# Spreading a bisection's sign passes over more steps of an attention mixer on one Trainium2 core

## Chip, cores and metric

One core of one Trainium2 chip runs the whole program. The metric is the time of one execution in device microseconds (us), median of several runs; lower is better.

## What is computed

The reference is two transformer blocks in sequence, in fp32, on 1024 tokens of width 1024 with a context of 256 tokens. The first block has two layers (latent attention, a depthwise convolution, a Fourier branch and a spatial gate). The second has a hybrid mixer with three kinds of attention, a memory attention and a convolutional feed-forward. The change lies in the third kind of attention of the mixer: for each query an index score is computed against every earlier key, and only the 256 best keys are attended to.

```python
score = jnp.einsum('bqhk,bqh->bqk', jax.nn.relu(logits), iwb)
score = jnp.where(kpos[None, None, :] <= qpos[None, :, None], score, NEG)
_, idx = lax.top_k(score, topk)            # topk = 256
...
s = jnp.where(valid[:, None], s + bias, NEG)
p = jax.nn.softmax(s, axis=-1)
```

## The kernel before

The queries of the mixer are eight tiles of 128 (t = 0 to 7); tile t sees (t+1)*128 keys. The mixer runs as 64 steps. Step n belongs to branch n // 16 and, in it, to query tile (n % 16) // 2 and to one of two head pairs. Branches 0 and 1 (steps 0 to 31) are the difference attention, branch 2 (steps 32 to 47) is the dilated one, and branch 3 (steps 48 to 63) is the one with the selected keys. So steps 0, 1, 16, 17, 32, 33, 48 and 49 are the narrowest and 14, 15, 30, 31, 46, 47, 62 and 63 the widest.

Each engine has its own program, written out by hand, in which the steps follow one another; engines meet at semaphores. In one step n:

- TensorE (PE) multiplies the scores of step n (`scores2`, L934), transposes the probabilities of step n-1 (`turn2`, L945), runs **fillers** (projections for the next branch, L856 and L867, half of the output projection, L879), transposes the output of an earlier step back (`back2`, L972), and multiplies with the values of step n-1 (`values2`, L957 or L962).
- VectorE (DVE) adds the bias and takes the row maximum (`scored`, L2172), narrows the search (`narrow`, L2056 to L2071), adds the two maps of a head pair (`combine`, up to step 31) or scales them (`normalise`, L2195 and L2197, from step 32), and, up to step 32, divides the output of the step before (`divide`, L2210).
- ScalarE (ACT) copies transposes out of PSUM (`turned2`, L1145), takes the exponentials (`weigh`, L1560, two a step), copies fillers out, copies the output of the step before (with a root of its mean square up to step 32, `head_root`, L1568 to L1573), and counts signs (`count_signs`, L1604 and L1607). It also issues the DMAs of the bias strips, behind steps 16, 31, 46 and 47.

PE may issue the scores of a step before the softmax of the step before is done, since there are four PSUM banks for scores; fillers share two banks and transposes two more.

**The search.** The 256th largest score of every row is found by bisection on the bits of the number, in 33 passes. A pass of a tile is one ACTIVATE with the function Sign over the whole tile and its sum (L1607; pass 0 is L1604), and then four or so tiny VectorE instructions for all tiles of the group at once (`narrow`). The next pass needs the bound that the last one gave. Tiles 2 to 5 are the group "low" (widths 384, 512, 640 and 768), tiles 6 and 7 the group "high" (896 and 1024). In ACT's program tiles 2 and 3 are counted behind the first exponential of the step, and tiles 4 to 7 behind the second. VectorE narrows for pass n-1 in step n.

A pass used to come in every step: low in steps 0 to 32, high in steps 23 to 55. When a group is done, `keep_ranked` (L2108 to L2133) makes the mask of one tile out of the bound, one tile at a time, on VectorE alone and at the end of a step: it counts the scores above the bound, finds which of several equal scores are kept, by a running sum over parts of 256, and writes the mask over the scores. The table `RANKED_AT` says behind which step each tile is ranked: tiles 2, 3, 4 and 5 behind 34, 36, 38 and 40, tiles 6 and 7 behind 57 and 59. The masks are first read by `scored` of step 52 (tile 2), 54 (tile 3), 56, 58, 60 and 62.

Fillers stand in steps 0 to 47, in step 52 (the mean square of the memory tokens, L886) and from step 54 on. Steps 48 to 51 and 53 have none.

```python
for piece in FILLERS.get((n, 1), ()):
    filled(*piece)
...
keep_ranked(n)
if 1 <= n <= 32:
    divide(n - 1)
```

Of the kernel before, what the change touches and what calls it, by code (L numbers as in the profile page):

```python
# [205 lines left out]


SEARCHED = {"low": (2, 3, 4, 5), "high": (6, 7)}
SEARCH_AT = {"low": 0, "high": 23}
PASSES = 33  # L210
RANKED_AT = {34: 2, 36: 3, 38: 4, 40: 5, 57: 6, 59: 7}
MEM_STEP = 52
FILLERS = fillers()
INDEX_FILLERS = projections(0, ("k0", "q0", "k1", "q1", "v"))
# [51 lines left out]
class Psum:  # L266
# [20 lines left out]
    def at(self, key):  # L287
        return self.tensor[:, self.bank[key] * 512:8 * 512]
# [48 lines left out]
def program(nc, A, known):  # L337
# [94 lines left out]
    def sel(t):  # L432
        return view(SEL_AT[t], (t + 1) * P)
# [704 lines left out]
    def scalar_program(raw):  # L1138
# [452 lines left out]

        def count_signs(group, n, tiles):

            i = n - SEARCH_AT[group]
            if not 0 <= i < PASSES:
                return
            for t in tiles:
                j, x = t - 2, sel(t)
                out = signs_out[t % 2][:, 0:(t + 1) * P]
                e.wait_ge(*at(unread_signs.get(t % 2)))  # L1600
                unread_signs[t % 2] = ("counted", group, i, t)
                if i == 0:
                    e.wait_ge(*at(("causal", t)))
                    ins = act(out, x, ACT.Sign, accum_out=tally[:, j:j + 1])  # L1604
                else:
                    e.wait_ge(*at(("bound", group, i)))
                    ins = act(out, x, ACT.Sign, bias=bound[:, j:j + 1], scale=sense[:, j:j + 1],  # L1607
                              accum_out=tally[:, j:j + 1])
                ins.then_inc(*e.step(("counted", group, i, t)))
# [4 lines left out]
        for n in range(STEPS2 + 1):  # L1614
            if n >= 1:
                turned2(n - 1, 0)
            if n < STEPS2:
                weigh(n, 0)
            count_signs("low", n, (2, 3))
            for piece in FILLERS.get((n, 0), ()):  # L1620
                filled(*piece)
            if n >= 33:
                turned2(n - 1, 1)
            if n < STEPS2:
                weigh(n, 1)
            count_signs("low", n, (4, 5))
            count_signs("high", n, (6, 7))
            for piece in FILLERS.get((n, 1), ()):
                filled(*piece)
# [78 lines left out]
    def vector_program(raw):  # L1708
# [321 lines left out]
        v.tensor_scalar(subln8, vec("subln"), 1.0 - LAM_INIT, None, ALU.mult).then_inc(*e.step("subln8"))  # L2030
        def narrow(group, n):

            i = n - SEARCH_AT[group]
            if not 0 <= i < PASSES:
                return
            tiles = SEARCHED[group]
            g = slice(tiles[0] - 2, tiles[-1] - 1)
# [52 lines left out]
        def parts_of(t):  # L2090
            return [(a, min(256, (t + 1) * P - a)) for a in range(0, (t + 1) * P, 256)]

        def keep_ranked(n):

            if n not in RANKED_AT:
                return
            t = RANKED_AT[n]
            j, x, parts = t - 2, sel(t), parts_of(t)
# [37 lines left out]
        for t, i in INDEX_STEPS:  # L2136
            for m in range(2):
                h = 2 * i + m
                n = 8 * (t - 2) + h
# [81 lines left out]
        for n in range(STEPS2 + 1):  # L2221
            if n < STEPS2:
                scored(n, 0)
            narrow("low", n - 1)
            if n < STEPS2:
                scored(n, 1)
            narrow("high", n - 1)
            for piece in FILLERS.get((n, 0), ()):
                filled(*piece)
            if n < 32:  # L2230
                combine(n)
            elif n < STEPS2:
                normalise(n, 0)
                normalise(n, 1)
            for piece in FILLERS.get((n, 1), ()):
                filled(*piece)
            if n == MEM_STEP:
                e.wait_ge(*at("mem rr"))
                for k in range(KD):
                    stt(out=mem[:, k, :], in0=mem[:, k, :], scalar=vec("norm_memkv", k), in1=mem_rr, op0=ALU.mult,  # L2240
                        op1=ALU.mult).then_inc(*e.step(("mem h", k)))
# [3 lines that stand above are left out]
# [416 lines left out]
```

## Time and profile before

| what | value |
|---|---|
| median of 3 runs | 3642.03 us (3641.57 to 3643.51) |
| profiled execution, its own time | 3638.48 us |
| its span, first to last instruction | 3636.3 us |
| PE busy | 3475.0 us (96%) |
| PE weight loads | 1830.7 us (50%) |
| DVE busy | 1456.9 us (40%) |
| ACT busy | 1008.1 us (28%) |
| mean granted TensorE clock | 0.983 of full |

The profiled execution is 3.55 us below the median of the runs, and its time is 2.2 us above its span. The mixer's 64 steps lie between 1774.6 and about 2426.8 us from the span's start. Step starts used below are those of the first scores matmul of a step on PE.

### The profile page before, as it was taken

How to read it: one execution, taken by the hardware profiler on the slowest of the kernel's cores; microseconds unless marked ns; L12 is line 12 of the kernel's file. 1: busy time of each engine (PE TensorE's matmuls, PEld its weight loads, DVE VectorE, ACT ScalarE, POOL GpSimd, SP SyncE). 2: the span in 40 equal slices, each digit the busy share in tenths (PEclk: the TensorE clock that was granted, in tenths of full speed). 3: DMA queues.
4: the chain of work that ended last, by engine and by line, in shares of the span. 5: the costliest groups of instructions: out<-in, count | busy, mean ns of one | idle time of the engine just before them, and what ended most of it. 6: DMA issues, size and time to landing. Idle time of an engine off the chain costs nothing.

```text
span 3636.3 us, 31117 instructions
## 1 busy us (share of the span) xinstructions
PE 3475.0 (96%) x12466; PEld 1830.7 (50%) x12466; DVE 1456.9 (40%) x2652; ACT 1008.1 (28%) x2122; POOL 70.4 (2%) x91
## 2 busy tenths in 40 slices
PE   7999999999999999999999899899999999999998
PEld 3556555655456445444566455564544444444443
DVE  2056191123056351232443363652224555153433
ACT  4244112002244111112688745531211000000001
POOL 0000000010000000100000000000000000000000
PEclk9999999999999999999999999899999999999999
DMA  5100121130000101111100101111001111111111
GB/s 212 50 5 12 58 86 61 52 113 32 26 6 13 39 26 47 47 38 41 41 24 24 38 21 61 56 44 49 24 18 40 41 41 45 36 46 41 41 41 64
DMA packets 49901, 163.70 MB, mean 45 GB/s; under 512 B 5296, under 2 KB 8624, under 8 KB 49085
## 3 DMA queue, kind: packets, MB, share of 16 engines
q1 hardware_dynamic: 44890, 145.82, 11.5%
q10 hardware_dynamic: 4868, 15.91, 1.3%
q8 instruction: 98, 1.61, 0.2%
q14 instruction: 45, 0.37, 0.0%
HBM read 157.46 MB, written 11.32 MB: 46 GB/s over the span
## 4 chain that ended last, share of the span: by engine, by line
PE 86%; DVE 6%; ACT 6%; issue 1%; SPq 1%; DMA 0%; POOL 0%; DVEq 0%; ACTq 0%; POOLq 0%
PE ps L485 43%; PE ps L1086 14%; PE ps L856 5%; PE ps L576 4%; PE ps L867 2%; ACT sb L1607 2%; PE ps L599 2%; PE ps L755 2%; PE ps L588 2%; PE ps L879 1%; PE ps L934 1%; PE ps L945 1%; DVE sb L1795 1%; PE ps L841 1%; ACT sb L1560 1%; PE ps L962 1%
## 5 line engine op out<-in xcount | busy, mean ns | idle before, releaser
L485 PE MATMUL ps<-sb 128*128 128x512 f32 (+1 forms) x3856 | 1568.6, 568 | 13.6 <-ACT sb L1410 6.7
L485 PEld LDWEIGHTS ps<-sb 128*128 128x128 f32 x3856 | 733.7, 191 | 840.3 <-issue 820.9
L1145 ACT ACTIVATE sb<-ps 128x512 f32<-128x512 f32 (+11 forms) x706 | 349.2, 511 | 1434.0 <-PE ps L485 542.3
L1086 PE MATMUL ps<-sb 128*128 128x512 f32 x1232 | 529.9, 592 | 2.9 <-DVE sb L2353 2.9
L1086 PEld LDWEIGHTS ps<-sb 128*128 128x128 f32 x1232 | 233.9, 190 | 298.2 <-issue 292.7
L856 PE MATMUL ps<-sb 128*128 128x512 f32 x512 | 232.9, 603 | 0.0
L1187 ACT ACTIVATE sb<-sb 128x512 f32<-128x512 f32 x128 | 76.0, 613 | 479.7 <-DVE sb L1997 157.6
L1607 ACT ACTIVATE sb<-sb 128x384 int8<-128x384 f32 (+2 forms) x192 | 184.4, 963 | 1.0 <-DVE sb L2052 0.5
L1931 DVE SCALAR_TENSOR_TENSOR sb<-sb 128x1310 f32<-128x1310 f32 (+1 forms) x120 | 161.7, 1432 | 0.0
L576 PE MATMUL ps<-sb 96*128 96x512 f32 (+1 forms) x400 | 155.3, 523 | 5.2 <-ACT sb L1319 4.5
L856 PEld LDWEIGHTS ps<-sb 128*128 128x128 f32 x512 | 94.9, 193 | 108.3 <-issue 107.5
L1795 DVE TENSOR_REDUCE sb<-ps 128x1 f32<-128x1280 f32 (+1 forms) x72 | 98.9, 1373 | 97.4 <-PE ps L576 97.1
L1720 DVE SCALAR_TENSOR_TENSOR sb<-sb 128x512 f32<-128x512 f32 (+1 forms) x138 | 88.0, 706 | 110.8 <-ACT sb L1168 86.0
L2300 DVE TENSOR_TENSOR sb<-ps,sb 128x512 f32<-128x512 f32 x64 | 44.3, 691 | 216.6 <-PE ps L485 216.6
L867 PE MATMUL ps<-sb 128*128 128x256 f32 x512 | 118.5, 387 | 0.0
L1560 ACT ACTIVATE sb<-sb 128x128 f32<-128x128 f32 (+7 forms) x128 | 98.7, 771 | 62.2 <-DVE sb L2172 33.1
L576 PEld LDWEIGHTS ps<-sb 96*128 96x128 f32 x400 | 71.9, 192 | 78.8 <-issue 73.2
L867 PEld LDWEIGHTS ps<-sb 128*128 128x128 f32 x512 | 97.7, 195 | 18.9 <-issue 6.2
L588 PE MATMUL ps<-sb 128*128 128x128 f32 x656 | 99.5, 281 | 5.1 <-DVE sb L1812 2.1
L1319 ACT ACTIVATE sb<-ps,sb 128x1280 f32<-128x1280 f32 (+1 forms) x72 | 88.7, 1232 | 48.9 <-DVE sb L1795 48.7
L1997 DVE SCALAR_TENSOR_TENSOR sb<-ps,sb 128x512 f32<-128x512 f32 (+1 forms) x40 | 27.9, 697 | 176.2 <-PE ps L485 176.2
L945 PE MATMUL ps<-sb 128*128 128x128 f32 x432 | 70.9, 288 | 28.8 <-DVE sb L2210 18.7
(225 smaller groups left out, 2872.9 us busy)
## 6 DMA issues: line engine op xcount, KB each, us to landing
sb<-in_w_in SPq DMA_DIRECT2D x73, 512.0 KB, 3.3
sb<-in_w_ada SPq DMA_DIRECT2D x48, 512.0 KB, 4.6
sb<-in_w_up SPq DMA_DIRECT2D x44, 512.0 KB, 3.3
sb<-in_w_down SPq DMA_DIRECT2D x24, 384.0 KB, 3.0
sb<-in_w_out SPq DMA_DIRECT2D x16, 512.0 KB, 3.3
sb<-in_w_mkv SPq DMA_DIRECT2D x16, 512.0 KB, 3.3
rows_dram<-vec_dram ACTq DMA_DIRECT2D x1, 6906.0 KB
sb<-rows_dram ACTq DMA_DIRECT2D x6, 1024.0 KB, 5.3
```

Source lines behind the costliest of these rows:

```text
L485: ins = mm(ps[:, 0:tn], w[:, k, :], src(k, t0, tn), start=(k == 0), stop=(k == nk - 1))
L576: ins = mm(ps[:, b:b + w], qh[0:96, h % 2, t * P:(t + 1) * P], kh[0:96, h, keys0 + b:keys0 + b + w], start=True, stop=True)
L588: ins = transpose(ps[:, (j - g) * P:(j - g + 1) * P], prob[u % 3][:, j * P:(j + 1) * P], ident)
L856: ins = mm(ps[:, 0:512], weights[name][:, k, :], H2[:, k, 512 * c:512 * c + 512], start=(k == 0), stop=(k == KD - 1))
L867: ins = mm(ps[:, 0:256], H2[:, k, t * P:(t + 1) * P], w[k // 4][:, k % 4, :], start=(k == 0), stop=(k == KD - 1))
L945: ins = transpose(ps[:, (j - g) * P:(j - g + 1) * P], score_tile(n, m)[:, j * P:(j + 1) * P], ident)
L1086: ins = mm(ps[:, 0:512], stationary(k), moving(k), start=(first and k == 0), stop=(k == 3), skip_group_check=not first)
L1145: return act(out, in_, func, scale=scale)
L1560: act(tile, tile, ACT.Exp, bias=small[:, s:s + 1], scale=-1.0, accum_out=small[:, s + 1:s + 2]).then_inc(*e.step(("exp2", n, m)))
L1607: ins = act(out, x, ACT.Sign, bias=bound[:, j:j + 1], scale=sense[:, j:j + 1], accum_out=tally[:, j:j + 1])
L1795: v.tensor_reduce(small[:, s:s + 1], psum.at((l, "s", u))[:, 0:nk], AX.X, ALU.max, negate=True).then_inc(*e.step((l, "max", u)))
L1931: ins = stt(out=out, in0=src, scalar=w, in1=out, op0=ALU.mult, op1=ALU.add)
```

## The change

Two tables of step numbers replace the two first steps. Pass i of the low group now stands in step 4*i // 3 and pass i of the high group in step 12 + 4*i // 3, so a group has passes in three steps of four and none in the steps with n % 4 == 3. Low: steps 0, 1, 2, 4, 5, 6, ... 42. High: 12, 13, 14, 16, ... 54. The two groups leave out the same steps. The rankings of tiles 2 to 5 move to the ends of steps 45, 46, 48 and 50; those of tiles 6 and 7 stay. Nothing is added or taken away; the number of passes is 33 for both groups as before.

```diff
 SEARCHED = {"low": (2, 3, 4, 5), "high": (6, 7)}
-SEARCH_AT = {"low": 0, "high": 23}
 PASSES = 33
-RANKED_AT = {34: 2, 36: 3, 38: 4, 40: 5, 57: 6, 59: 7}
+SEARCH_AT = {group: {first + 4 * i // 3: i for i in range(PASSES)} for group, first in (("low", 0), ("high", 12))}
+RANKED_AT = {45: 2, 46: 3, 48: 4, 50: 5, 57: 6, 59: 7}
```

In `count_signs` and in `narrow` alike:

```diff
-            i = n - SEARCH_AT[group]
-            if not 0 <= i < PASSES:
+            i = SEARCH_AT[group].get(n)
+            if i is None:
                 return
```

The first place is ACT's program in step 20 (branch 1, tile 2), from its first exponential to the root of the output of step 19. Before:

```order
L1560 ACTIVATE sb<-sb 128x384
L1607 ACTIVATE sb<-sb 128x384
L1607 ACTIVATE sb<-sb 128x512
L1560 ACTIVATE sb<-sb 128x384
L1607 ACTIVATE sb<-sb 128x640
L1607 ACTIVATE sb<-sb 128x768
L1568 ACTIVATE sb<-ps,sb 128x128
L1571 ACTIVATE sb<-sb 128x1
L1573 ACTIVATE sb<-sb 128x1
```

The same place in the changed kernel:

```order
L1560 ACTIVATE sb<-sb 128x384
L1607 ACTIVATE sb<-sb 128x384
L1607 ACTIVATE sb<-sb 128x512
L1560 ACTIVATE sb<-sb 128x384
L1607 ACTIVATE sb<-sb 128x640
L1607 ACTIVATE sb<-sb 128x768
L1607 ACTIVATE sb<-sb 128x896
L1607 ACTIVATE sb<-sb 128x1024
L1568 ACTIVATE sb<-ps,sb 128x128
L1571 ACTIVATE sb<-sb 128x1
L1573 ACTIVATE sb<-sb 128x1
```

Two wide signs have come in front of the root; in step 19, just before, all four signs are gone.

The second place is VectorE's program between step 48 and step 49 (branch 3, tile 0; ISA is `scored`). Before, from the last scaling of step 48:

```order
L2195 RECIPROCAL sb<-sb 128x1
L2197 TENSOR_SCALAR sb<-sb 128x128
L2172 ISA sb<-ps,sb 128x128
L2172 ISA sb 128x1
L2172 ISA sb<-ps,sb 128x128
L2172 ISA sb 128x1
```

In the changed kernel, from the same scaling:

```order
L2195 RECIPROCAL sb<-sb 128x1
L2197 TENSOR_SCALAR sb<-sb 128x128
L2108 TENSOR_SCALAR sb<-sb 128x256 x2
L2108 TENSOR_SCALAR sb<-sb 128x128
L2108 TENSOR_SCALAR sb<-sb 128x256 x2
L2108 TENSOR_SCALAR sb<-sb 128x128
L2110 TENSOR_SCALAR sb<-sb 128x1
L2112 TENSOR_TENSOR sb<-sb 128x1
L2113 TENSOR_SCALAR sb<-sb 128x1
L2115 SCALAR_TENSOR_TENSOR sb<-sb 128x1
L2118 SCALAR_TENSOR_TENSOR sb<-sb 128x1
```

Thirteen rows more of the same ranking (tile 4) follow, up to L2133, before `scored` of step 49. The ranking of tile 5 stands in the same way between steps 50 and 51.

## Rows read from the trace of the kernel before

**Rows 1.** The page, part 1: busy time of each engine over the whole span
```profile
PE 3475.0 (96%) x12466; PEld 1830.7 (50%) x12466; DVE 1456.9 (40%) x2652; ACT 1008.1 (28%) x2122; POOL 70.4 (2%) x91
```
**Rows 2.** Busy time by stretch: steps 0-11, 12-15, 16-19, 20-23, 24-27, 28-31, 32-38
```profile
core 0: us, PE busy (x) PEld busy (x) DVE busy (x) ACT busy (x) POOL busy (x), PEclk, DMA share, GB/s
1774.60:1867.60 93.00, 88.96 (x391) 57.72 (x390) 38.40 (x162) 79.69 (x218) 0.29 (x1) 1.00 0.13 46
1867.60:1907.60 40.00, 38.65 (x169) 21.61 (x168) 19.66 (x52) 32.37 (x77) 0.00 (x0) 1.00 0.06 20
1907.60:1937.10 29.50, 28.06 (x107) 14.77 (x106) 9.90 (x52) 25.01 (x73) 0.00 (x0) 1.00 0.18 64
1937.10:1967.40 30.30, 29.56 (x137) 20.85 (x136) 13.08 (x52) 27.31 (x76) 0.00 (x0) 1.00 0.06 18
1967.40:2014.30 46.90, 37.71 (x178) 27.18 (x178) 18.43 (x72) 40.38 (x99) 0.00 (x0) 0.93 0.06 23
2014.30:2062.60 48.30, 42.23 (x169) 22.91 (x168) 21.73 (x68) 41.96 (x95) 0.00 (x0) 0.93 0.06 16
2062.60:2137.00 74.40, 73.78 (x329) 47.20 (x328) 33.30 (x149) 41.16 (x104) 0.00 (x0) 1.00 0.10 33
```
**Rows 3.** Busy time of the sign passes alone (L1607): steps 0-11, steps 44-47
```profile
1774.60:1867.60 93.00, 39.64 (x88) 1.00 0.13 46
2212.70:2267.80 55.10, 9.78 (x16) 1.00 0.15 51
```
**Rows 4.** Busy time by stretch: steps 25, 27, 29, 31, and the sum over 24-31
```profile
1974.50:1992.30 17.80, 13.43 (x58) 10.74 (x57) 5.79 (x21) 13.46 (x33) 0.00 (x0) 0.81 0.00 0
...
2000.00:2014.30 14.30, 10.98 (x46) 5.92 (x46) 5.93 (x19) 13.68 (x32) 0.00 (x0) 1.00 0.19 74
...
2021.60:2037.60 16.00, 13.11 (x48) 6.81 (x47) 6.44 (x19) 13.16 (x30) 0.00 (x0) 0.89 0.11 33
...
2045.70:2062.60 16.90, 13.75 (x51) 7.30 (x50) 7.03 (x19) 15.05 (x33) 0.00 (x0) 0.90 0.06 14
sum 95.20, PE 79.93 PEld 50.09 DVE 40.16 ACT 82.34 POOL 0.00; mean PE 9.99 PEld 6.26 DVE 5.02 ACT 10.29 POOL 0.00
```
**Rows 5.** Timeline, step 24 into 25: start, us, engine, line [idle <-releaser]
```profile
1977.79 1.23 ACT L1607 ACTIVATE sb<-sb 128x1024 int8<-128x1024 f32 x1
...
1980.08 0.20 ACT L1573 ACTIVATE sb<-sb 128x1 f32<-128x1 f32 x1
...
1980.39 0.41 DVE L2210 TENSOR_SCALAR sb<-ps,sb 128x128 f32<-128x128 f32 x1 [4.04 <-ACT sb L1573]
...
1980.85 0.47 PE L945 MATMUL ps<-sb 128*128 128x128 f32 x1 [3.80 <-DVE sb L2210]
```
**Rows 6.** Busy time by stretch: step 39 and step 41
```profile
2137.00:2155.90 18.90, 15.38 (x56) 6.92 (x54) 14.11 (x45) 5.22 (x11) 0.00 (x0) 0.91 0.05 15
...
2166.10:2187.10 21.00, 16.84 (x64) 8.07 (x62) 15.23 (x45) 5.76 (x13) 0.00 (x0) 0.84 0.10 26
```
**Rows 7.** Timeline of DVE: first and last row of the rankings of tiles 4, 5
```profile
2136.87 0.47 DVE L2108 TENSOR_SCALAR_CACHE_REDUCE sb<-sb 128x256 f32<-128x256 f32 x1
...
2146.47 0.49 DVE L2133 TENSOR_SCALAR sb<-sb 128x640 f32<-128x640 f32 x1
...
2165.75 0.47 DVE L2108 TENSOR_SCALAR_CACHE_REDUCE sb<-sb 128x256 f32<-128x256 f32 x1
...
2176.23 0.56 DVE L2133 TENSOR_SCALAR sb<-sb 128x768 f32<-128x768 f32 x1
```
**Rows 8.** Timeline of steps 48 to 52: ends of scalings, next `scored`, memory sum
```profile
2272.10 0.29 DVE L2197 TENSOR_SCALAR sb<-sb 128x128 f32<-128x128 f32 x1
...
2273.59 0.29 DVE L2172 CUSTOM_DVE_ANT_0 sb<-ps,sb 128x128 f32<-128x128 f32 x1 [1.21 <-PE ps L934]
...
2279.63 0.35 DVE L2197 TENSOR_SCALAR sb<-sb 128x256 f32<-128x256 f32 x1
...
2280.94 0.42 DVE L2172 CUSTOM_DVE_ANT_0 sb<-ps,sb 128x256 f32<-128x256 f32 x1 [0.95 <-PE ps L934]
...
2287.97 6.75 PE L886 MATMUL ps<-sb 128*128 128x256 f32 x16 [1.37 <-ACT sb L1647]
```

More of the change, by code:

```diff
@@ L2031, in narrow @@
         def narrow(group, n):
-            i = n - SEARCH_AT[group]
-            if not 0 <= i < PASSES:
+            i = SEARCH_AT[group].get(n)
+            if i is None:
                 return
```

## The prediction

> **What bounds the kernel.** I read the page's busy times first. PE is busy for 3475.0 us of a span of 3636.3 [rows 1], so outside its idle time and its slow clock nothing can be won without less work, and the change takes no work away. The question is only what it does to PE's idle time and clock in the mixer. So I cut the mixer into stretches of four steps, since the new tables repeat every four, and took busy time and granted clock of each [rows 2], the sign passes alone [rows 3], the odd steps in which both groups run [rows 4], the chain behind one stall [rows 5], and the places where a ranking stands or will stand [rows 6 to 8].
>
> What the reader is to see: in steps 0 to 23, with the low group alone, PE idles for 4.0 us of 93.0, then 1.4, 1.4 and 0.7 us [rows 2]. In steps 24 to 31, with both groups, it idles for 9.2 and 6.1 us and the clock falls to a mean of 0.93, which means half speed (1.2 of 2.4 GHz) for a seventh of the 95.2 us, 13.6 us, or 6.8 us lost. Of these 15.3 us of idle time 13.7 lie in the odd steps 25, 27, 29 and 31 (4.4, 3.3, 2.9 and 3.2) [rows 4]. Rows 5 show the chain: six signs, then the root, then the division on DVE, which was idle for 4.04 us behind ACT's L1573, and then PE, idle for 3.80 us. ACT is not full there (82.3 of 95.2); it is the order in its queue that costs: what PE needs stands behind the signs.
>
> From step 32 on PE has more work a step and the signs cost nothing: in steps 32 to 38 PE is busy for 73.8 of 74.4 us, with one step of both groups and two rankings in it [rows 2]. The rankings of tiles 4 and 5 do cost: steps 39 and 41 hold 3.5 and 4.2 us of idle time, at clocks of 0.91 and 0.84 [rows 6].
>
> **The change part by part.** All times are against the profiled execution's 3638.48 us; the same difference is then put on the median, 3642.0, which is 3.5 higher.
>
> *A. Low passes in steps 0 to 11, nine instead of twelve.* A low pass takes ACT 39.64 / 11 = 3.6 us (88 rows are eleven passes of eight), a high one 9.78 / 4 = 2.45 us [rows 3]. Steps 3, 7 and 11 lose their 3.6 us. At best all 4.0 us of idle time go, at worst none. Two of six odd-step stalls go with their signs and the others start with less behind them. I take -2.5.
>
> *B. Both groups in 15 of the steps 12 to 31, none in five.* Before, the low group was in all 20 and the high one in 9. Three ways to price this from rows:
> - Each four steps are bound by ACT's work plus the 0.75 us a step that ACT idled in steps 20 to 23 (30.3 - 27.3, over four), or by PE. A stretch with three passes of both instead of four low ones has 18.15 - 14.4 = 3.75 us more ACT work. So 16-19 becomes 25.0 + 3.75 + 3.0 = 31.8 (2.3 more), 20-23 34.1 (3.8 more), 12-15 stays at 40; 24-27 has 18.15 in place of 24.2 and becomes 37.3 (9.6 less), 28-31 likewise 38.9 (9.4 less). Sum: -12.9.
> - Each step with both costs what the eight of 24-31 cost on average over PE's full-speed work, (95.2 - 79.9 + 6.8) / 8 = 2.8 us. Then 15 x 2.8 = 42 stand against 22.1 plus the 3.5 of steps 12 to 23 before: +16.
> - The cost falls on the odd steps with both, as rows 4 show. The new table has five of them (13, 17, 21, 25, 29) where there were four, and 20.5 / 4 x 5 = 25.6 us stand against the same 25.6 before: 0.
>
> I take 0, because rows 4 are the nearest: they show where in a pair the loss falls. The ends are -13 and +16.
>
> *C. Low passes in nine of the steps 33 to 42.* 9 x 3.6 = 32 us more on ACT, in a stretch where it is busy for little over half the time [rows 2]. The cover is the fillers; the one step with both in it left 0.6 us of idle time in seven steps. At worst 0.6 for each, +5.6; at best 0. I take +1.
>
> *D. The rankings leave steps 38 and 40.* Step 39 ran at half speed for 0.18 of 18.9 us, so its full-speed work is 15.4 - 1.7 = 13.7 and 5.2 us come back. Step 41: 0.32 of 21.0 at half speed, work 16.8 - 3.4 = 13.5, and 7.5 come back [rows 6]. Together -12.7. Tiles 2 and 3 cost nothing behind 34 and 36 and, I think, nothing behind 45 and 46, where PE's steps are longer; should both hold one DVE step too long, the end is +3.
>
> *E. The rankings arrive in steps 48 and 50.* They take DVE 2146.96 - 2136.87 = 10.1 and 2176.79 - 2165.75 = 11.0 us [rows 7], and here there are no fillers. In order:
> - The last scaling of step 48 ends at 2272.4. With the ranking behind it, `scored` of step 49 starts at 2282.5 and not at 2273.6: 8.9 late [rows 8].
> - From there to the last scaling of step 50 there were 6.4 us (2273.59 to 2279.98). The signs of step 49 stay in front of the exponentials, those of step 48 are now under the ranking: 8.6 late.
> - The second ranking ends at 2280.0 + 8.6 + 11.0 = 2299.6, where `scored` of step 51 stood at 2280.9: 18.7 late.
> - From there to the memory sum of step 52 there were 7.0 us. The high signs of step 51 are gone (2.45) and those of step 50 lie under the ranking (I put their last 0.6 here): 15.6 late.
>
> I take +15.5, with ends of 12 (all three passes of 48, 50 and 51 hidden or gone in full) and 19 (nothing hidden). Whoever stands behind: scores and transposes of step 49 on PE, the exponentials on ACT, and through them every step to 52. The clock was already at a mean of 0.78 here before the change.
>
> *F. At nothing:* step 55 loses a high pass under fillers; the strips' DMAs behind steps 16, 31, 46 and 47 are used at least one step later than issued and move by one pass at most; SP's weight loads follow PE; `narrow` moves with its pass.
>
> Sum: -2.5 + 0 + 1 - 12.7 + 15.5 = **+1.3 us**, 3639.8 on the profiled time and 3643.3 on the median. A measurement of this kernel tells apart some 0.2%, 7.3 us: faster means below 3634.7, slower above 3649.3.
>
> **The skill against the rows.** Rows 4 show half speed in three of four odd stalls, but none in step 27, with 3.3 us of idle time. The Trainium skill, TensorE: Matmul & The Clock Gate, section "HAM oscillation", says that waits which recur in a loop put the array back on its slow clock every time. By that rule stalls that are spread over steps 13 to 29 pay for it as often as those that stood close together; by that rule part B is at 0 or above, and step 27 is against it. The same skill's Perfetto Trace Analysis, section "Optimization Strategy", advises to interleave regimes whose busiest engine differs, which this change does with its ACT-heavy and PE-heavy steps. That speaks for the first rival.
>
> **Rivals.**
> 1. *The free step takes up the backlog.* Each fourth step has no signs, and what ACT owes from the three before is paid there under PE's fillers. B is then -12.9: 3630.4. For it: ACT is busy for only 87% of steps 24 to 31. Against it: rows 5, a stall right behind the second step with both. Chance 0.14.
> 2. *The narrow steps pay, slower.* In 16, 17, 18, 20, 21 and 22 PE has 28 to 30 us for four steps, and three passes of both take 18 of them; ACT becomes the longer one in each, and the root and division of the step wait behind six signs. It decides as soon as ACT's queue from one exponential to the next root is longer than PE's step. Every step with both then costs its 2.8 us, B is +16: 3659. For it: ACT had only 3.0 of 30.3 us left in steps 20 to 23. Against it: nearly all the loss lay in odd steps. Chance 0.18.
> 3. *The slow clock outlasts the rankings.* PE has little to do for 27 us instead of 12, and half speed reaches on past the memory sum, for one of the lengths seen (3.4 in step 39, 6.7 in step 41): +3.4 at most, 3646.7. Chance 0.10.
> 4. *The freed steps fill up again.* The low signs in 37, 38, 40, 41 and 42 stand before the copies that PE waits for, C is at its upper end (4.6 more) and so are tiles 2 and 3 of D (3.0 more): 3651. Chance 0.08.
> 5. *The change does not do what it says:* the idle time of 39 and 41 was not the ranking's and stays, +14: 3656. Rows 7 put the ranking exactly there. Chance 0.02.
>
> My forecast has the remaining 0.48: 3643.3, with its own spread of about 4 us to each side.
>
> **How the numbers follow.** Faster takes rival 1 and a little of the forecast's lower edge: 0.15. Slower takes rivals 2 and 5 and half of 4 with a little of the upper edge: 0.25. The rest is 0.60. The range 3630 to 3656 takes in all cases but rival 2, so it leaves out 0.18; its lower end is rival 1, its upper end rival 5.
>
> **What would show it.** Step 39 and 41 without idle time and at clock 1.0. DVE busy without a break for 10 and 11 us between steps 48 and 51, with PE idle, and the memory sum some 15 us later against the start of step 48. In steps 12 to 23 PE's idle time at odd steps up from 3.5 us to about 13, in 24 to 31 down from 15.3 to about 8, and hardly any in steps 15, 19, 23, 27 and 31. The forecast is wrong if the gain of 24 to 31 is not eaten by 12 to 23, or if the steps 48 to 51 cost less than 12 us.

## The result, and the profile after

The changed kernel takes 3656.59 us (median of 6 runs, 3653.6 to 3658.56) beside 3641.82 us for the kernel before (6 runs, 3640.49 to 3643.82). The ratio is 1.0038, with a 95% interval of 1.0027 to 1.0048. That is 14.8 us more, and twice the 7.3 us below which the prediction called it no change; it had given the side above that, slower, a chance of 0.25. The profiled execution took 3658.56 us, with a span of 3656.6 us.

The page, part 1, of the changed kernel; the row that answers is [rows 1]:

```profile
PE 3480.8 (95%) x12466; PEld 1834.1 (50%) x12466; DVE 1456.6 (40%) x2652; ACT 1008.3 (28%) x2122; POOL 70.3 (2%) x91
```

The work is the same. The profiled executions are 20.3 us apart in span, since one lies 3.3 us below its median and the other 2.0 above. Of this 13.7 us lie in the mixer, where PE is busy for 1.5 us less (593.3 and 594.8) and idle for 15.2 us more (72.6 and 57.4). The other 6.6 us, and the whole of the 5.8 us by which the page has PE busier, lie outside the mixer, in code that the change does not touch.

The same stretches as in [rows 2] and [rows 6], of the changed kernel: steps 0-11, 12-15, 16-19, 20-23, 24-27, 28-31, 32-38, then step 39 and step 41:

```profile
1779.80:1872.40 92.60, 88.92 (x391) 57.71 (x390) 37.14 (x153) 69.92 (x194) 0.29 (x1) 1.00 0.13 46
1872.40:1918.40 46.00, 40.31 (x172) 22.46 (x170) 20.55 (x65) 35.58 (x81) 0.00 (x0) 0.96 0.05 17
1918.40:1951.50 33.10, 29.63 (x105) 15.30 (x104) 11.03 (x60) 28.62 (x78) 0.00 (x0) 0.95 0.16 57
1951.50:1987.10 35.60, 31.30 (x137) 22.04 (x136) 14.14 (x60) 30.88 (x81) 0.00 (x0) 0.95 0.05 15
1987.10:2032.70 45.60, 38.06 (x179) 26.84 (x178) 17.39 (x61) 33.56 (x82) 0.00 (x0) 0.93 0.07 24
2032.70:2080.60 47.90, 41.85 (x171) 22.92 (x170) 20.61 (x60) 35.94 (x81) 0.00 (x0) 0.93 0.05 17
2080.60:2154.90 74.30, 73.68 (x327) 47.11 (x326) 20.29 (x99) 54.19 (x139) 0.00 (x0) 1.00 0.11 33
2154.90:2168.30 13.40, 13.40 (x54) 6.42 (x52) 5.77 (x20) 4.07 (x10) 0.00 (x0) 1.00 0.08 20
2178.50:2192.60 14.10, 14.10 (x64) 7.25 (x62) 6.16 (x19) 10.37 (x25) 0.00 (x0) 1.00 0.14 38
```

Steps 12 to 15 grew from 40.0 to 46.0 us, 16 to 23 from 59.8 to 68.7, and in all three stretches of four the clock fell below 1.00. ACT is busier there by 3.2, 3.6 and 3.6 us, and PE's steps grew by 6.0, 3.6 and 5.3. Steps 24 to 31 gave back little: 95.2 became 93.5 us, although ACT now has 69.5 us of work there and had 82.3. Steps 32 to 38 kept their length with 13 us more work on ACT. Steps 39 and 41 are without idle time at full clock, 5.5 and 6.9 us shorter.

The end of the mixer, of the changed kernel: steps 44-47, 48-51 and 52-63, and its 64 steps as a whole:

```profile
2218.20:2273.30 55.10, 55.10 (x284) 29.48 (x282) 31.74 (x90) 26.57 (x52) 0.00 (x0) 1.00 0.15 50
2273.30:2307.10 33.80, 12.42 (x91) 7.67 (x89) 27.41 (x104) 14.87 (x42) 0.00 (x0) 0.63 0.20 74
2307.10:2445.70 138.60, 118.72 (x763) 91.46 (x761) 90.43 (x224) 60.27 (x134) 0.00 (x0) 0.90 0.16 54
1779.80:2445.70 665.90, 593.29 (x2882) 375.35 (x2881) 320.25 (x1069) 425.40 (x1040) 0.29 (x1) 0.94 0.12 40
```

and of the kernel before:

```profile
2212.70:2267.80 55.10, 55.10 (x282) 29.46 (x281) 19.32 (x50) 28.91 (x56) 0.00 (x0) 1.00 0.15 51
2267.80:2284.30 16.50, 11.48 (x90) 7.33 (x88) 8.94 (x48) 15.50 (x43) 0.00 (x0) 0.78 0.40 147
2284.30:2426.80 142.50, 121.22 (x763) 93.30 (x761) 91.58 (x232) 63.84 (x142) 0.00 (x0) 0.88 0.15 52
1774.60:2426.80 652.20, 594.77 (x2882) 376.01 (x2881) 320.06 (x1069) 424.70 (x1040) 0.29 (x1) 0.95 0.12 41
```

Tiles 2 and 3 fit under steps 45 and 46 (55.1 us both times). In steps 48 to 51 PE's two longest waits are 8.64 and 9.62 us, each for a copy of transposes that comes late behind a ranking. The sum over the mixer: -0.4 (steps 0-11), +13.2 (12-31), -12.5 (32-43), 0 (44-47), +17.3 (48-51), -3.9 (52-63), together +13.7 us. The mixer itself began at 1774.6 us in one execution and at 1779.8 in the other. Over the fourteen profiled executions of this study that start lies between 1774.6 and 1781.5 whatever the kernel, so kernels are compared below by mixer steps and by medians, not by profiled ends.

The rankings, timeline of DVE in steps 48 to 52 of the changed kernel, with the memory sum of step 52; the rows that answer are [rows 7, 8]:

```profile
2277.64 0.29 DVE L2197 TENSOR_SCALAR sb<-sb 128x128 f32<-128x128 f32 x1
...
2287.45 0.49 DVE L2133 TENSOR_SCALAR sb<-sb 128x640 f32<-128x640 f32 x1
2287.86 0.28 DVE L2172 CUSTOM_DVE_ANT_0 sb<-ps,sb 128x128 f32<-128x128 f32 x1
...
2304.10 0.56 DVE L2133 TENSOR_SCALAR sb<-sb 128x768 f32<-128x768 f32 x1
2304.57 0.41 DVE L2172 CUSTOM_DVE_ANT_0 sb<-ps,sb 128x256 f32<-128x256 f32 x1
...
2309.33 3.89 PE L886 MATMUL ps<-sb 128*128 128x256 f32 x16
```

The `scored` of step 49 starts as soon as the ranking of tile 4 is through, and that of step 51 behind the ranking of tile 5. Against the start of step 48 they are 8.8 and 18.2 us later than before, where the prediction said 8.9 and 18.7. The memory sum starts 2309.33 - 2273.3 = 36.0 us after step 48 began, and before it was 2287.97 - 2267.8 = 20.2: 15.9 us later, where the prediction said some 15.

What the prediction did not see coming, timeline of steps 14 and 15 of the changed kernel. Step 15 has no sign pass at all:

```profile
1900.15 1.72 PE L957 MATMUL ps<-sb 128*128 128x128 f32 x14
...
1902.12 1.01 ACT L1607 ACTIVATE sb<-sb 128x768 int8<-128x768 f32 x1
...
1903.13 1.12 ACT L1607 ACTIVATE sb<-sb 128x896 int8<-128x896 f32 x1
...
1904.25 1.23 ACT L1607 ACTIVATE sb<-sb 128x1024 int8<-128x1024 f32 x1
...
1905.95 0.35 ACT L1568 ACTIVATE sb<-ps,sb 128x128 f32<-128x128 f32 x1
...
1907.06 0.41 DVE L2210 TENSOR_SCALAR sb<-ps,sb 128x128 f32<-128x128 f32 x1 [3.86 <-ACT sb L1573]
...
1907.53 1.12 PE L945 MATMUL ps<-sb 128*128 128x128 f32 x4 [3.15 <-DVE sb L2210]
```

PE has the output of step 13 ready at 1901.87. Its root (L1568) stands on ACT behind the two high signs of step 14 (widths 896 and 1024), the last of which ends at 1905.48, and starts at 1905.95. The division on DVE waits for the root, and PE's next transposes wait for the division: in the code they want a PSUM bank that is free only after it. PE is idle for 3.15 us in step 15, and the loss shows in an odd step without signs, while the signs that cause it are those of the even step before. All even steps from 12 to 30 have a high pass in the new table. It leaves out only steps 15, 19, 23, 27 and 31, which are odd.

In the narrow steps another instruction of ACT stands in that place. Timeline of step 22 of the changed kernel:

```profile
1969.12 1.23 ACT L1607 ACTIVATE sb<-sb 128x1024 int8<-128x1024 f32 x1
...
1970.60 0.46 ACT L1587 ACTIVATE sb<-ps,sb 128x256 f32<-128x256 f32 x1
...
1971.21 0.52 PE L945 MATMUL ps<-sb 128*128 128x128 f32 x3 [3.89 <-ACT sb L1587]
```

L1587 is `back`, which empties the bank of the output that was turned back. ACT has it in every odd step, behind all signs of that step. So the waits of PE of over 2 us in steps 12 to 31 fall in steps 13, 15, 25, 27, 29 and 31 (2.52, 3.15, 3.53, 3.31, 2.88, 3.15 us behind the root) and in 18 and 22 (2.85 and 3.89 us behind `back`).

### The profile page after: what moved, and what is told of

Its sections match the earlier page's. It is cut to its first block, busy times and chain, and to the rows that moved or that the text cites. A ratio compares the mean times of both kernels' runs of the same rounds, so it can differ in the third digit from the quotient of the medians.

```text
span 3656.6 us, 31116 instructions
## 1 busy us (share of the span) xinstructions
PE 3480.8 (95%) x12466; PEld 1834.1 (50%) x12466; DVE 1456.6 (40%) x2652; ACT 1008.3 (28%) x2122; POOL 70.3 (2%) x91
## 3 DMA queue, kind: packets, MB, share of 16 engines
q1 hardware_dynamic: 44890, 145.82, 11.5%
## 4 chain that ended last, share of the span: by engine, by line
PE 86%; DVE 6%; ACT 5%; issue 1%; SPq 1%; DMA 0%; POOL 0%; DVEq 0%; ACTq 0%; POOLq 0%
PE ps L485 42%; PE ps L1086 14%; PE ps L856 5%; PE ps L576 4%; PE ps L867 3%; PE ps L599 2%; ACT sb L1607 2%; PE ps L755 2%; PE ps L588 2%; PE ps L879 2%; PE ps L934 1%; PE ps L945 1%; DVE sb L1795 1%; PE ps L962 1%; PE ps L841 1%
## 5 line engine op out<-in xcount | busy, mean ns | idle before, releaser
L485 PE MATMUL ps<-sb 128*128 128x512 f32 (+1 forms) x3856 | 1565.8, 567 | 13.5 <-ACT sb L1410 6.7
L1607 ACT ACTIVATE sb<-sb 128x384 int8<-128x384 f32 (+2 forms) x192 | 184.3, 962 | 1.2 <-DVE sb L2052 0.5
```

What stands on the lines that cost most here:

```text
L485: ins = mm(ps[:, 0:tn], w[:, k, :], src(k, t0, tn), start=(k == 0), stop=(k == nk - 1))
```

## The experiments

**Theory 1, the place in the queue.** What costs is that high signs stand on ACT ahead of the root, and it costs where PE has nothing else to do, behind even steps. **Theory 2, the load.** What costs is how much sign work a step holds, and a step with both groups pays wherever the signs stand. Each edit moves work and leaves none out. A number behind a time is its ratio to the kernel before, with the 95% interval. The kernel before, run beside them, had medians of 3639.8 to 3641.4 us.

**The change in parts: high table alone, low table alone.**

```
-SEARCH_AT = {"low": 0, "high": 23}                      (the kernel before)
+SEARCH_AT = {"low": {i: i ...}, "high": {12 + 4 * i // 3: i ...}}        e1_high_only, rankings as before
+SEARCH_AT = {"low": {4 * i // 3: i ...}, "high": {23 + i: i ...}}        e2_low_only, rankings at 45, 46, 48, 50
```

> The high group alone gets the new steps (12 to 54, three of four); the low group stays in steps 0 to 32 and the rankings behind 34, 36, 38, 40. Theory 1, the root behind the signs: an odd step stalls when the even step before it has high signs, since the root of the output waits behind them and holds a PSUM bank; the low passes make no difference. Then steps 12 to 31 take as long as in the changed kernel (208 us, 13 more than before) and the rest is as before: about 3655 us. Theory 2, ACT's load: what counts is the work of ACT per four steps. Here the low group has its full 20 passes in steps 12 to 31, five more (18 us) than in the changed kernel: steps 12 to 31 at 215 us or more, 3662 us or more.

> The low group alone gets the new steps (0 to 42, three of four) with the rankings behind 45, 46, 48 and 50; the high group stays in steps 23 to 55. Theory 1: steps 12 to 31 as before (195 us), since the same even steps, 24 to 30, carry high signs; steps 32 to 43 lose the 12.5 us of the two rankings, and steps 48 to 52 gain 14 to 17 us, a little more than in the changed kernel because step 51 keeps its high signs: 3642 to 3647 us. Theory 2: steps 24 to 31 fall by 4 to 5 us, since ACT has two low passes less there: 3638 to 3642 us.

Measured: 3658.31 us for the high table alone (ratio 1.0044, interval 1.0029 to 1.0059), 3641.28 for the low table with its rankings (0.9997, 0.9987 to 1.0007). Steps 12-23 and 24-31 of the high table alone:

```profile
1874.50:1994.30 119.80, 104.36 (x409) 61.30 (x408) 47.48 (x196) 104.59 (x262) 0.00 (x0) 0.93 0.08 27
1994.30:2086.40 92.10, 78.47 (x348) 49.27 (x346) 39.24 (x129) 76.34 (x180) 0.00 (x0) 0.94 0.06 21
```

Together 211.9 us. The high table carries the whole loss of steps 12 to 31, and load adds to it: with the low group in every step the stretch is 3.7 us longer than with it in three of four. The low table alone leaves 12 to 31 at 192.4 us (195.0 before), 2.2 us of the gain in 24 to 31. Taken by themselves these two runs do not decide. The first lies about midway between the theories (208 and 215 us for the stretch, 3655 and 3662 for the time), and the second gained 2.2 us in 24 to 31, where theory 1 expected none and theory 2 expected 4 to 5; its time is in theory 2's range and 0.7 us below theory 1's. What points to theory 1 are the waits: the low table took the low signs out of steps 27 and 31, and PE still waits 3.31 and 3.15 us there, as before.

**The rankings under steps with fillers.** The change's tables, with `RANKED_AT = {43: 2, 44: 3, 45: 4, 46: 5, 57: 6, 59: 7}`.

> The changed kernel with the rankings of tiles 2 to 5 behind steps 43, 44, 45 and 46, all under fillers, in place of 45, 46, 48 and 50. If the rankings' price in steps 48 to 52 is the missing fillers alone, those steps fall back by 13 to 17 us. The ranking of tile 5 behind step 46 delays the first score of step 47 by some 9 us, which step 47 (16 us of PE work) hides in part: 3 to 6 us of idle time there. Together 7 to 13 us below the changed kernel: 3644 to 3650 us. The rival is that a ranking costs its 5 to 8 us wherever it stands, as in steps 39 and 41 before: then no more than 4 us below the changed kernel.

Measured: 3640.71 us (0.9996, 0.9986 to 1.0005), below what was expected: 3 to 6 us of idle time had been set down for step 47. Steps 44-47 and 48-51:

```profile
2216.20:2272.10 55.90, 55.14 (x282) 29.46 (x280) 49.66 (x148) 26.07 (x52) 0.00 (x0) 1.00 0.16 55
2272.10:2288.50 16.40, 11.40 (x91) 7.29 (x88) 9.07 (x45) 14.88 (x43) 0.00 (x0) 0.83 0.35 132
```

Two rankings of 10 and 11 us cost 0.8 us behind steps 45 and 46, and 17.3 us in steps 48 to 51. So term E of the prediction is confirmed as a cause. Term D, what steps 39 and 41 win, is confirmed by the two runs before this one: the first kept the rankings behind 38 and 40 and kept the waits (3.51 and 4.15 us), the second moved them and lost the waits. With the rankings covered the change is back at no difference, because the loss of steps 12 to 31 and the gain of 39 and 41 are of one size.

**The root ahead of the high signs.** On the change, in even steps up to 32 the root goes between the low signs of tiles 4 and 5 and the high signs. It so comes to stand ahead of the high signs and also of the copies of the fillers that follow them.

```
             count_signs("low", n, (4, 5))
+            early = n % 2 == 0 and 2 <= n <= 32
+            if early:
+                head_root(n - 1)
             count_signs("high", n, (6, 7))
...
-            if 1 <= n <= 32:
+            if 1 <= n <= 32 and not early:
                 head_root(n - 1)
```

> The changed kernel with one move in ACT's program: in even steps up to 32 the root of the last step's output stands in front of the two high signs and not behind them (and behind the fillers' copies). Nothing else moves. Theory 1: the stalls of 2.5 to 3.9 us in steps 13, 15, 18, 22, 25, 27, 29 and 31 go for the most part, with the slow clock that follows them; steps 12 to 31 fall from 208 us to 185 to 193 us, and the time to 3634 to 3643 us. Theory 2, ACT's load: the same work in another order, no more than 3 us less. It could also cost, where ACT then waits in order for PE's values before it may count: up to 1 us a step.

Measured: 3634.39 us (0.9979, 0.9968 to 0.9989), 22 us less than the change with the same passes in the same steps. Steps 12-23 and 24-31:

```profile
1870.80:1978.70 107.90, 99.84 (x411) 59.06 (x410) 46.09 (x185) 93.77 (x238) 0.00 (x0) 0.97 0.09 30
1978.70:2057.40 78.70, 73.49 (x345) 46.59 (x344) 38.03 (x121) 68.30 (x163) 0.00 (x0) 1.00 0.07 25
```

186.6 us where the change had 208.2. The same place as above, end of step 14 (the division is L2213 here, since three lines stand before it):

```profile
1900.19 0.35 ACT L1568 ACTIVATE sb<-ps,sb 128x128 f32<-128x128 f32 x1
...
1901.10 1.12 ACT L1607 ACTIVATE sb<-sb 128x896 int8<-128x896 f32 x1
1901.30 0.41 DVE L2213 TENSOR_SCALAR sb<-ps,sb 128x128 f32<-128x128 f32 x1 [1.03 <-ACT sb L1573]
1901.76 0.66 PE L945 MATMUL ps<-sb 128*128 128x128 f32 x4 [0.33 <-DVE sb L2213]
...
1929.85 0.45 PE L945 MATMUL ps<-sb 128*128 128x128 f32 x1 [2.43 <-ACT sb L1587]
```

The stall of 3.15 us is down to 0.33, and steps 24 to 31 run at full clock. The last row, in step 18, is the other kind, which this edit does not touch: `back` behind the signs of step 17. By stretch the edit gave 46.0 - 40.4 = 5.6 us in steps 12-15, 93.5 - 78.7 = 14.8 in 24-31, and 68.7 - 67.5 = 1.2 in 16-23, where 7.7 us above the kernel before remain. Putting `back` ahead too was not tried.

**The same load in odd or in even steps.** The low group in every step and the rankings as before; ten high passes in the odd steps 13 to 31 or in the even steps 12 to 30.

```
+SEARCH_AT = {"low": {i: i ...}, "high": {n: i for i, n in enumerate([*range(13, 32, 2), *range(32, 55)])}}   e5_high_odd
+SEARCH_AT = {"low": {i: i ...}, "high": {n: i for i, n in enumerate([*range(12, 31, 2), *range(32, 55)])}}   e6_high_even
```

> The kernel before with the 33 high passes in the ten odd steps 13 to 31 and in every step 32 to 54; low passes, rankings and ACT's order as before. Theory 1 (the stall comes from the high signs of an even step, behind which the root of the step before waits): no step 12 to 31 has high signs in an even step, so these steps take 185 to 195 us, less than the 195.0 of before, and the time is 3630 to 3640 us. Theory 2, ACT's load: ten high passes in steps 12 to 31 where before had nine: 195 us or a little more, 3642 us.

> As the kernel with high passes in odd steps, but they stand in the ten even steps 12 to 30. The number of passes and ACT's work are the same. Theory 1: ten even steps with high signs and low signs in every step, so every step behind one stalls, at 2 to 4 us each and partly with the slow clock: steps 12 to 31 take 205 to 215 us, and the time is 3652 to 3662 us. Theory 2: the same as with the odd steps, within 3 us.

Measured: 3628.28 us (0.997, 0.9955 to 0.9985) with odd, 3649.91 (1.0024, 1.001 to 1.0037) with even steps. Sums over steps 12-23 and 24-31, odd:

```profile
sum 186.20, PE 171.62 PEld 104.37 DVE 83.19 ACT 168.13 POOL 0.00; mean PE 85.81 PEld 52.19 DVE 41.60 ACT 84.06 POOL 0.00
```

and even:

```profile
sum 205.60, PE 179.29 PEld 108.44 DVE 84.15 ACT 169.20 POOL 0.00; mean PE 89.64 PEld 54.22 DVE 42.07 ACT 84.60 POOL 0.00
```

ACT is busy for 168.1 and 169.2 us, the stretch takes 186.2 and 205.6: equal load, 19.4 us apart. With high signs in even steps all six waits are there again (13, 15, 25, 27, 29 and 31, of 2.51 to 3.80 us); with high signs in odd steps none of them is over 1.5 us. Both times lie a little below the expected ranges (3628.3 and 3649.9), the lengths within them.

But the 19.4 us are not spread evenly. They are 7.3 in steps 12 to 15 (40.0 and 47.3 us) and 13.3 in 24 to 31 (79.8 and 93.1). In the narrow steps 16 to 23 the place makes no such difference. Odd, then even:

```profile
1910.60:1977.00 66.40, 59.41 (x240) 36.13 (x241) 25.21 (x120) 59.60 (x162) 0.00 (x0) 0.97 0.10 36
1920.30:1985.50 65.20, 59.47 (x243) 36.20 (x242) 23.98 (x116) 58.88 (x160) 0.00 (x0) 0.97 0.11 37
```

Both are 5 to 7 us above the 59.8 us of before, with ACT busy for nine tenths of the stretch. In both PE waits 2.23 us in step 20 behind `back`. With high signs in even steps alone, `back` stands there behind low signs and a copy:

```profile
1951.57 1.01 ACT L1607 ACTIVATE sb<-sb 128x768 int8<-128x768 f32 x1
...
1953.06 0.46 ACT L1587 ACTIVATE sb<-ps,sb 128x256 f32<-128x256 f32 x1
...
1953.66 0.41 PE L945 MATMUL ps<-sb 128*128 128x128 f32 x2 [2.23 <-ACT sb L1587]
```

So theory 1 holds for the wide steps, and in the narrow ones the extra load costs in either place.

**The root first in the kernel before.** The edit of the fourth run, with the old tables.

> The kernel before with the root of the last step's output in front of the high signs in even steps up to 32, and nothing else changed. Theory 1: steps 24 to 31 fall from 95.2 us to 79 to 83, as in the changed kernel with the same move (78.7, with low passes in six of the eight); the rest stays: 3626 to 3631 us. If the spread itself were worth something beside the order, this kernel would be slower than that in steps 24 to 31.

Measured: 3626.64 us (0.9962, 0.995 to 0.9975), and steps 24 to 31 take 82.5 us in place of 95.2. The wait was in the kernel all along. The change did not make it; it put it under more steps. Two more things can be read here. Steps 12 to 23, which hold only one high pass, take 99.1 us in place of 99.8, so the root's place ahead of the fillers' copies is worth little by itself. And the spread is worth something in the wide steps once the order is mended: the changed table with the same edit took 78.7 us in 24 to 31, and here 2.25 us of waiting behind `back` come up in step 32, so that 32 to 38 take 78.1 us and not 74.4.

**Both repairs, then smaller pieces of ranking.** The eighth run takes the tables of the change, the covered rankings and the early root. The ninth also cuts the rankings of tiles 6 and 7, which stood whole behind steps 57 and 59, into pieces behind steps 55 to 61. An entry is a tile, its first part and the part it stops before; the first entry of a tile brings its counts. `keep_ranked` is split to match, which is not shown.

```
+RANKED_AT = {43: [(2, 0, 9)], 44: [(3, 0, 9)], 45: [(4, 0, 9)], 46: [(5, 0, 9)], 55: [(6, 0, 1)], 56: [(6, 1, 2)],
+             57: [(6, 2, 9)], 58: [(7, 0, 0)], 59: [(7, 0, 2)], 60: [(7, 2, 3)], 61: [(7, 3, 9)]}
```

> The changed kernel with both repairs: the root in front of the high signs in even steps, and the rankings behind steps 43 to 46. If the two costs are apart, the gains add: 22 us of the first and 16 us of the second below the changed kernel, 3617 to 3622 us, the mixer 625 to 629 us. Less than 30 us together would mean that they share a cause.

> The changed kernel with both repairs (root in front of the high signs in even steps, tiles 2 to 5 ranked behind steps 43 to 46), and the rankings of tiles 6 and 7 cut into pieces: the counts and one part, or one or two parts of 256, behind each of the steps 55 to 61, in place of one whole ranking behind 57 and one behind 59. The work is the same. A whole one delays the next step's scores by 11 to 13 us and leaves PE idle for 5.2 and 7.1 us at steps 58 and 60, with slow clock; pieces of 5 to 7 us should be hidden in steps of 9 to 10 us in part: steps 56 to 63 fall from 105 us to 88 to 98, and the time to 3601 to 3611 us. The rival: VectorE's total work there (71 of 105 us) and the chain from score to probability are what bounds, and the pieces only spread the stall: no more than 3 us less.

Measured: 3617.03 us (0.9937, 0.9922 to 0.9952) and 3599.5 us (0.9893, 0.9876 to 0.9909), the second 1.5 us below its range. The gains add: 15.9 us for the rankings and 22.2 for the root against the change, and 39.6 for both. Steps 56-59 and 60-63 of the ninth run:

```profile
2298.00:2337.30 39.30, 36.52 (x252) 29.20 (x250) 34.63 (x92) 16.45 (x40) 0.00 (x0) 1.00 0.23 81
2337.30:2387.30 50.00, 49.05 (x363) 39.10 (x361) 33.38 (x57) 22.88 (x48) 0.00 (x0) 1.00 0.18 64
```

Steps 56 to 59 took this of the kernel before:

```profile
2322.00:2366.90 44.90, 38.35 (x251) 30.43 (x248) 34.88 (x95) 16.46 (x40) 0.00 (x0) 0.92 0.21 71
```

With about as much work of DVE (34.6 and 34.9 us) the pieces leave PE idle for 2.8 us and at full clock, where it idled for 6.5 at 0.92. Between the eighth and the ninth run, which differ in the pieces alone, steps 56 to 63 fell from 105.1 to 89.3 us.

**Three other tables on top.** Ranking pieces and early root stay. e10 has the high group in steps 4 to 43 (up to 31 in three of four) and the low one in 0 to 32; e11 the old dense tables, with high from 22; e12 the odd pattern of e5. In all three the rankings of tiles 2 to 5 stand in steps 34 to 41, those of 4 and 5 in two pieces.

> As the kernel with split rankings, but the high group is searched in steps 4 to 43 (three of four to step 31, then every step) and the low group in steps 0 to 32 as before; so tile 6 and the counts of tile 7 are ranked behind steps 44 to 46, under fillers, and tiles 2 to 5 behind 34 to 41, tiles 4 and 5 in two pieces each. No signs stand in steps 48 to 55. Steps 4 to 11 pay for the high signs (2 to 4 us), steps 12 to 31 for denser low signs (2 to 4 us), steps 33 to 47 stay without idle time, steps 48 to 63 lose 5 to 10 us against the split version. Together 3595 to 3608 us. If the load of ACT decided in steps 4 to 31 after all, they would lose more than 10 us and this kernel would be slower than the split one.

> The pass tables of before (low in every step 0 to 32; high in every step 22 to 54), the root first in even steps, the rankings of tiles 4 and 5 in two pieces in steps 38 to 41, those of 6 and 7 in the pieces of e9. Theory 1 (the place in ACT's queue costs, and the wide stretches of DVE): 12-23 takes 100 to 104 us where e9 took 107.8, 24-31 about 83 (as in e7) where it took 78.7, 32-43 138 to 140, 48-51 about 16.5; mixer 608 to 614, time 3595 to 3602, so the changed tables were worth nothing once the order is mended. Rival (the changed tables help once the order is mended): 24-31 and 32-43 together take 10 us or more above e9's 216.3, time 3606 or more.

> As e11, but the high group in the odd steps 13 to 31 and in all of 32 to 54. Theory 1: high signs never stand ahead of a root in an even step, so 24-31 takes 79 to 82 us; 12-23 pays for six high passes under dense low ones, 102 to 107; the rest as e11: mixer 607 to 613, time 3594 to 3601, a tie with e11 within 4 us. Rival (the load counts, not the place): five high passes less in 24-31 give 6 us or more there against e11 and six more in 12-23 cost the same again.

Measured: 3603.8 (0.9901, 0.9886 to 0.9915), 3604.1 (0.99, 0.9885 to 0.9915) and 3603.26 us (0.9894, 0.9878 to 0.9911); none beats the ninth run's 3599.5, and the intervals overlap. Steps 12-23, 24-31 and 32-43 of e11:

```profile
1870.70:1969.80 99.10, 96.32 (x411) 57.26 (x410) 43.06 (x164) 85.61 (x227) 0.00 (x0) 1.00 0.10 32
1969.80:2053.50 83.70, 75.47 (x345) 47.71 (x344) 40.24 (x137) 80.42 (x190) 0.00 (x0) 0.98 0.06 23
2053.50:2196.00 142.50, 140.00 (x611) 80.97 (x610) 78.49 (x281) 72.08 (x171) 0.00 (x0) 0.98 0.10 33
```

Against the ninth run (107.8, 78.8, 137.6) this is 8.7 less, 4.9 more and 4.9 more. The last two make 9.8 us, just short of the 10 that the rival (the changed tables help once the order is mended) had asked for; the dense tables win it back in 12 to 23. So the tables trade narrow steps against wide ones. e11 missed its expectation in two places of the mixer: 12-23 took 99.1 where 100 to 104 were expected, and 32-43 took 142.5 for 138 to 140, with 2.5 us of idle time at step 32 and a slow clock behind it. e12 has four high passes more than e11 in 12-23 and four fewer in 24-31 (its expectation counted six and five), and took 6.2 us more and 3.5 less there. The 6.2 us lie in steps 16 to 23 (65.8 and 59.6 us), with two of the four passes; the two in steps 13 and 15 cost nothing (39.5 us in 12 to 15 both times). That is the narrow steps' price again, which no run here splits into load and `back`'s place. Both mixers came out above their ranges, 615.3 and 614.5 us, and both times too (3604.1 for at most 3602, 3603.26 for at most 3601). Some 3 us of it are in steps 52 to 63 (126.2 and 127.1 against 123.8), which hold the same passes as in the ninth run; 2.2 and 3.0 of that is in step 52 alone, where runs of equal work differ as well (last section). In e10 steps 4 to 11, with six high passes and two more low ones, took 72.8 us against the ninth run's 66.0, where 2 to 4 us more were expected.

## What was right in the prediction and what was wrong, point by point

The forecast was 3643.3 us, inside the band of no change; 3656.59 came, at the upper end of the range of 3630 to 3656 (the ratio of 1.0038 on the forecast's base of 3642.0 is 3655.9). That the range reaches so far is luck: its upper end stood there for rival 5, which did not come. By its own sum, +1.3 us against +13.7 in the mixer:

- **A**, -2.5 expected, -0.4 measured: near its worst end. Taking three low passes, 10.8 us of ACT's work, out gave back 0.4. The two longest waits there are the same in both kernels, in step 9 (1.20 and 1.19 us) and in step 11 (1.02), though step 11 lost its signs.
- **B**, 0 expected with ends of -13 and +16, +13.2 measured: **this is the step that failed**, and it alone is nearly the whole error. Of three ways to price it I took the third, "the cost falls on the odd steps with both, as rows 4 show". [Rows 4] do show where the loss falls. I read from them whose signs cause it, and [rows 5] already said otherwise: the root that L2210 waits for there stands behind the signs of step 24, an even step, and the stall is in step 25. Read so, the price goes by even steps with a high pass. In the wide steps that gives six places instead of four (in front of 13, 15, 25, 27, 29, 31), and those are the six that stalled. The fourth run (22 us from the order alone) and the fifth and sixth (20.6 us apart in the wide steps, at equal load) show it. The narrow steps 16 to 23, with 8.9 of the 13.2 us, do not follow that rule: they stalled in 18 and 22, behind `back`, and the fifth and sixth run put the price there on the added passes wherever they stand. The count behind the third way was off too: before, step 23 held both groups as well, so there were five such odd steps and not four, and step 23 had no wait of over 1 us.
- That steps 15, 19, 23, 27 and 31 would have "hardly any" idle time was wrong for the same reason: 15, 27 and 31 had 3.15, 3.31 and 3.15 us. PE's idle time in steps 12 to 23 came to 13.5 us, near the 13 foretold, but by luck: the 13 were for odd steps, and half of the 13.5 are the waits in the even steps 18 and 22. In 24 to 31 it came to 13.6 where 8 were foretold. Neither of the two signs by which the forecast was to be known as wrong came up: the gain of 24 to 31, 1.7 us, was eaten by 12 to 23, and steps 48 to 51 cost 17.3 us. Both signs looked only for a kernel faster than the forecast.
- **C** and **D**, +1 and -12.7 expected: steps 32 to 43 came to -12.5, of it -5.5 and -6.9 in steps 39 and 41. Right, and the first and second run show that the ranking was the cause. Tiles 2 and 3 cost nothing, as taken.
- **E**, +15.5 expected with ends of 12 and 19: the memory sum was 15.9 us late, and steps 48 to 63 together +13.4. Right up to the memory sum. The 3.9 us that steps 52 to 63 gave back were not foreseen and can't be put down to the change: the fifth and sixth run have the same work from step 32 on and differ there by 3.8 us (138.5 and 142.3, at clocks of 0.93 and 0.88). They are inside the prediction's spread of 4 us.
- **F** at nothing: steps 44 to 47 did not move.

Of the rivals the first (the free step takes up the backlog) is refuted. ACT did have less to do in 24 to 31, 69.5 us of 93.5, and PE waited all the same. The second (narrow steps pay) named 3659 us and was right where it looked: 16 to 23 grew by 8.9 us, of which only 1.2 went with the order of the root. But its rule, that each step with both pays 2.8 us, does not hold for 12 to 15 and 24 to 31, where the fourth run leaves no single wait over 1.02 us with all passes in place. The third, a slow clock that outlasts the rankings, did not come: steps 52 to 63 ran at 0.90, before at 0.88, and the memory sum took 3.89 us where it had taken 6.75. Nor did the fourth and fifth: steps 39 and 41 have no idle time, and 32 to 38 only 0.6 us.

The Trainium skill, TensorE: Matmul & The Clock Gate, section "HAM oscillation", was quoted for stalls that are paid again each time. Of the eight stalls six brought a stretch of half clock and two (step 13 with 2.52 us, step 29 with 2.88) did not. So the trace agrees in six of eight, and with B above 0, as that rule had it. Its Perfetto Trace Analysis, section "Optimization Strategy", advises to interleave regimes with different busiest engines. The change does that and lost. The fourth run kept the interleaving and mended the order, and that was worth 22 us; with it mended, interleaved and dense tables (ninth and eleventh run) are 4.6 us apart.

## What to carry to other kernels

A stall that shows in one step can be caused by work in the step before. Follow the releaser back to the instruction it waited behind in its engine's queue before counting how many steps have "the" cause, and look at that queue's order before spreading load: on the old tables, moving the root ahead of the 2.4 us of high signs gave 13.2 us, and the best table by itself, with high signs in odd steps, 11.5. In steps too short for the optional work, the order gave little (1.2 us of 8.9 in steps 16 to 23). Long optional work on DVE belongs under steps in which PE has fillers, and if a step is too short for it, in pieces.

## What had not been expected of the hardware

The granted clock does not go by a stall's length alone. In the changed kernel a stall of 3.15 us was followed by 3.4 us at half clock in step 15 and by 6.8 in step 31, one of 2.85 us in step 18 by 3.4, and one of 2.88 in step 29 by none. The stall of 3.31 us in step 27 is the same in both kernels: before, it had no slow clock [rows 4], and in the changed one it had 3.4 us. Likewise step 52 takes 9.3 us in the fifth run and 12.3 in the sixth, with the same instructions and 2.53 us of idle time in both. So about 4 us of a mixer's length here is not explained by its stalls, and differences of that size between single stretches were not read as effects. No run took apart what decides it.
